# Projections of the prompt begun on four channel chunks, with half of shift and scale

## The reference

```python
mod = (jax.nn.silu(c) @ w_ada + b_ada)[:, None, :]
shift1, scale1, gate1, shift2, scale2, gate2 = jnp.split(mod, N_MOD, axis=-1)
h = rmsnorm(x, g_attn) * (1 + scale1) + shift1
z = h @ w_in
u, q, k, v = jnp.split(z, [D_FOURIER, D_FOURIER + D_NA, D_FOURIER + 2 * D_NA], axis=-1)
```

## Time and profile before

| | before |
| --- | --- |
| median of three runs | 1675.43 us |
| the profiled execution | 1672.69 us |
| its span, first to last instruction | 1670.9 us |
| mean granted TensorE clock | 0.994 of full speed |
| TensorE busy | 1627.1 us, 97% |
| VectorE busy | 1052.8 us, 63% |
| ScalarE busy | 643.7 us, 39% |
| GpSimd busy | 173.1 us, 10% |
| `front`: first matmul of the loop behind the u tiles starts | 139.65 us |

### The profile page before, as it was taken

One profiled execution on the slowest core, in us unless ns is written; L12 is line 12 of the kernel. 1 busy time (PEld: TensorE's weight loads), 2 busy tenths in 40 slices (PEclk: granted clock), 3 DMA queues, 4 the chain that ended last, 5 costly groups with the idle time before them and its releaser, 6 DMA issues.

```text
span 1670.9 us, 20970 instructions
## 1 busy us (share of the span) xinstructions
PE 1627.1 (97%) x7939; PEld 1301.3 (78%) x7939; DVE 1052.8 (63%) x1679; ACT 643.7 (39%) x1121; POOL 173.1 (10%) x123
## 2 busy tenths in 40 slices
PE   5999999999999999999999999999999999999998
PEld 3767888866676888888888888888888877888887
DVE  3524888058968353444664698887878745668774
ACT  4512333158765243433332334333333424343330
POOL 0311222000000232100000000000000001314060
PEclk9999999999999999999999999999999999999999
DMA  9771010433220432543444234333333476767773
GB/s 349 286 239 46 26 38 26 90 59 34 57 89 26 166 137 101 156 137 113 140 135 145 73 120 119 114 96 118 95 95 95 156 266 239 251 221 266 251 249 99
DMA packets 222071, 230.63 MB, mean 138 GB/s; under 512 B 25271, under 2 KB 169873, under 8 KB 221849
## 3 DMA queue, kind: packets, MB, share of 16 engines
q1 hardware_dynamic: 221017, 226.21, 43.0%
q0 software_dynamic: 960, 3.15, 0.5%
HBM read 183.30 MB, written 46.02 MB: 137 GB/s over the span
## 4 chain that ended last, share of the span: by engine, by line
PE 61%; DVE 2%; DMA 2%; SPq 1%; ACT 0%; issue 0%; DVEq 0%; ACTq 0%
PE banks L99 20%; PE banks L101 20%; PE banks L100 20%; DMA a_raw<-fc_rows 1%; PE banks L2405 1%; SPq L1763 1%; DVE a_lo L2210 0%; DVE s_sum L2156 0%; DMA s_raw<-in_w_up 0%; DVE b_lo L2222 0%; DMA s_raw<-in_w_gate 0%; DVE s_lo L2166 0%; SPq L1733 0%; SPq L1744 0%; DMA fc_rows<-s_up 0%
## 5 line engine op out<-in xcount | busy, mean ns | idle before, releaser
L99 PE MATMUL banks<-b_hi,a_hi 128*128 128x512 f32 x462 | 181.8, 394 | 7.9 <-DVE b_lo L2222 4.0
L101 PE MATMUL banks<-b_hi,a_lo 128*128 128x512 f32 x462 | 181.5, 393 | 0.0
L100 PE MATMUL banks<-b_lo,a_hi 128*128 128x512 f32 x462 | 181.3, 392 | 0.0
L99 PE MATMUL banks<-h_hi,p_hi 128*128 128x512 f32 x352 | 138.5, 394 | 0.0
L101 PE MATMUL banks<-h_hi,p_lo 128*128 128x512 f32 x352 | 137.2, 390 | 0.0
L100 PE MATMUL banks<-h_lo,p_hi 128*128 128x512 f32 x352 | 137.0, 389 | 0.0
L99 PE MATMUL banks<-h_hi,s_hi 128*128 128x512 f32 x352 | 136.9, 389 | 0.0
L100 PE MATMUL banks<-h_lo,s_hi 128*128 128x512 f32 x352 | 136.9, 389 | 0.0
L101 PE MATMUL banks<-h_hi,s_lo 128*128 128x512 f32 x352 | 136.9, 389 | 0.0
L99 PE MATMUL banks<-h_hi,win_hi 128*128 128x512 f32 x336 | 132.4, 394 | 3.6 <-DVE h_lo L522 2.8
L101 PE MATMUL banks<-h_hi,win_lo 128*128 128x512 f32 x336 | 131.3, 391 | 0.0
(11 more groups left out here) (263 smaller groups left out, 3404.0 us busy)
## 6 DMA issues: line engine op xcount, KB each, us to landing
a_raw<-fc_rows SPq DMA_DIRECT2D x40, 704.0 KB, 4.6
b_raw<-in_w_down SPq DMA_DIRECT2D x77, 256.0 KB, 5.5
ada_rest<-in_w_ada SPq DMA_DIRECT2D x16, 1024.0 KB, 8.7
b_second<-in_w_down SPq DMA_DIRECT2D x55, 256.0 KB, 6.2
p_raw<-in_w_gate SPq DMA_DIRECT2D x22, 512.0 KB, 3.8
p_raw<-in_w_up SPq DMA_DIRECT2D x22, 512.0 KB, 4.0
s_raw<-in_w_gate SPq DMA_DIRECT2D x11, 1024.0 KB, 5.2
s_raw<-in_w_up SPq DMA_DIRECT2D x11, 1024.0 KB, 5.3
```

The source lines that it names most:

```text
L99: pe.matmul(out, lhs[0], rhs[0], start=start, stop=False)
L100: pe.matmul(out, lhs[0], rhs[1], start=False, stop=False)
L101: return pe.matmul(out, lhs[1], rhs[0], start=False, stop=stop)
```

## The change

The order of the modulation blocks becomes 0, 2, 1, 3, so that shift and scale of channel chunks 0 to 3 are complete after two blocks, and `coef_ready` goes up once for each half. Loads are issued as: x of the prompt in two halves, ada 0, ada 2, w_in 0 and 1, ada 1, w_in 2 and 3, ada 3, then x of chunks 1 and 2. TensorE turns four chunks of the prompt, makes two blocks and their columns (now in banks 6 and 7), turns the other four chunks, then does chunks 0 to 3 of pair 0, block 1, chunk 0 of pair 1, block 3, chunk 1 of pair 1, the two turns of rows, chunks 2 and 3 of pair 1, and then the second halves of pairs 0 and 1. Of the turns of chunk 1 two stand in pair 1 (steps 6 and 7) and six in pair 2 (steps 0 to 5); those of chunk 2 all stand in pair 3. `rest_products(0)` moves from the end of pair 1 to the end of pair 2; blocks 1 and 2 move from pair 2 to pair 3, 3 and 4 to pair 4, 5 and 6 to pair 5, and `mods(7)` stands behind pair 5. The turns of chunk 1 use banks 6 and 7. ScalarE loads the root's table right behind silu; it has `square(4)` ahead of the wait for the second half of the coefficients and of `modulate(4)`, squares 5 to 7 between modulations 5, 6 and 7, and squares 8 and 9 and evacuations 2 and 3 between `modulate(9)` and `modulate(10)`. Semaphore `wf_in` now also counts the second half of x, so a later wait is for 32.

```diff
-            load_x(0)
-            for j in range(AC):
-                sp.dma_start(ada[j][:], w_ada[:, 512 * j:512 * j + 512].rearrange("(k p) n -> p k n", p=128)
-                             ).then_inc(ada_in[j], 16)
-            for r in range(FT):
-                load_u(r)
+            load_x_half(0, x_in[0])
+            load_x_half(1, wf_in)
+            load_ada(0)
+            load_ada(2)
+            load_u(0)
+            load_u(1)
+            load_ada(1)
+            load_u(2)
+            load_u(3)
+            load_ada(3)
             load_x(1)
             load_x(2)
...
+            act.activation(stat[:, 1, 0:1], eps_t[:], ACT.Sqrt)
             for t in range(4):
                 square(t)
             root_x(0)
...
             act.wait_ge(coef_ready, 1)
-            act.wait_ge(parked, KT)
-            for n in range(KT):
-                modulate(n)
+            act.wait_ge(parked, FT)
+            modulate(0)
+            modulate(1)
+            park_x(4)
+            modulate(2)
+            park_x(5)
+            modulate(3)
+            park_x(6)
+            park_x(7)
             split_u(2)
             split_u(3)
-            for t in range(4, 8):
-                square(t)
+            square(4)
+            act.wait_ge(coef_ready, 2)
+            act.wait_ge(parked, KT)
+            modulate(4)
+            modulate(5)
+            square(5)
+            modulate(6)
+            square(6)
+            modulate(7)
+            square(7)
             root_x(1)
             evacuate_u(0)
             evacuate_u(1)
-            for n in range(KT, 2 * KT):
-                modulate(n)
-                if KT + 2 <= n < KT + 6:
-                    square(n - 2)
-            root_x(2)
+            modulate(8)
+            modulate(9)
+            square(8)
+            square(9)
             evacuate_u(2)
             evacuate_u(3)
-            for n in range(2 * KT, 2 * KT + 4):
+            modulate(10)
+            square(10)
+            modulate(11)
+            square(11)
+            root_x(2)
+            for n in range(12, 2 * KT):
                 modulate(n)
...
-            for j in range(AC):
-                pe.wait_ge(ada_in[j], 16)
-                if j >= 2:
-                    pe.wait_ge(mod_row, j - 1)
-                mod_products(ada[j], 6 + j % 2, 0, True, False)
-                mod_products(ada[j][:, 4:8], 6 + j % 2, 4, False, True).then_inc(mod_summed, 1)
-                if j == 0:
-                    for n in range(KT):
-                        turn_x(n)
-                else:
-                    turn_first(j - 1)
-            turn_first(AC - 1)
-            u_pair(0, lambda k: None)
-
-            def during_1(k):
-                turn_x(KT + k)
-                if k == KT - 1:
-                    rest_products(0)
-            u_pair(1, during_1)
+            for n in range(FT):
+                turn_x(n)
+            first_products(0)
+            first_products(1)
+            turn_first(0)
+            turn_first(1)
+            pe.wait_ge(vec_ready, 1)
+            for n in range(FT, KT):
+                turn_x(n)
...
+            u_pair(0, nothing, range(FT))
+            first_products(2)
+            u_pair(1, nothing, range(1))
+            first_products(3)
+            u_pair(1, nothing, range(1, 2))
+            turn_first(2)
+            turn_first(3)
+            u_pair(1, nothing, range(2, FT))
+            u_pair(0, nothing, range(FT, KT))
...
+            def during_1(k):
+                if k >= KT - 2:
+                    if k == KT - 2:
+                        pe.wait_ge(coef_ready, 2)
+                    turn_x(KT + k - 6)
+            u_pair(1, during_1, range(FT, KT))
+
+            def during_2(k):
+                if k < KT - 2:
+                    turn_x(KT + 2 + k)
+                if k == KT - 1:
+                    pe.wait_ge(t_ready, 2 * KT)
+                    rest_products(0)
+            u_pair(2, during_2)
+
+            TURNS_3 = ((0, 1), (2,), (3,), (), (4, 5), (6,), (7,), ())
+
+            def during_3(k):
+                if k == 0:
+                    pe.wait_ge(bank_free, 4)
+                for i in TURNS_3[k]:
+                    turn_x(2 * KT + i)
+                if k % 4 == 3:
+                    mods(1 + k // 4)
+            u_pair(3, during_3)
...
             def during_later(p, k):
-                if p in (2, 3) and k % 2:
-                    if p == 2 and k == 1:
-                        pe.wait_ge(bank_free, 4)
-                    turn_x(2 * KT + 4 * (p - 2) + k // 2)
                 if k % 4 == 3:
-                    m = 2 * p - 3 + k // 4
-                    if m < CHUNKS:
-                        mods(m)
-            for p in range(2, U_TILES // 2):
+                    mods(2 * p - 5 + k // 4)
+            for p in range(4, U_TILES // 2):
                 u_pair(p, lambda k: during_later(p, k))
+            mods(CHUNKS - 1)
             turn_rest(CHUNKS - 1)
             pe.wait_ge(gate_ready, 4)
```

More of the change, by code:

```diff
@@ L159, in front @@
     x = at("x_first", [128, TT, D], F32, X_AT)
-    ada = [at(f"ada{j}", [128, KT, 512], F32, H_LO + 16384 * j if j < 3 else W + 8192) for j in range(AC)]
+    ADA_ORDER = (0, 2, 1, 3)
+    ADA_AT = {0: H_LO, 2: H_LO + 16384, 1: H_LO + 32768, 3: W + 8192}
+    ada = [at(f"ada{j}", [128, KT, 512], F32, ADA_AT[j]) for j in range(AC)]
     park = at("park", [128, KT, T], F32, H_HI)
@@ L364, in _ @@
             store(1)
-            for n in range(KT + 1, 2 * KT, 2):
+            low(9)
+            store(2)
+            store(3)
+            for n in range(11, 2 * KT, 2):
                 low(n)
[L367 to L374, removed]
+            store(4)
+            store(5)
+            for n in range(2 * KT + 1, 3 * KT, 2):
+                low(n)
             for n in range(6, U_TILES):
@@ L391, in square @@
                     act.wait_ge(x_in[t // 4], 16)
+                if t == 2:
+                    act.wait_ge(wf_in, 16)
                 if t:
@@ L462, in _, with park_x @@
             root_x(0)
-            for k in range(KT):
+            def park_x(k):
                 act.wait_ge(x_turned, k + 1)
                 act.activation(park[:, k, 0:CH], banks[:, x_bank(k)], ACT.Copy).then_inc(parked, 1)
+            for k in range(FT):
+                park_x(k)
             split_u(0)
@@ L489, in _ @@
             evacuate_u(5)
-            for n in range(2 * KT + 4, 3 * KT):
+            for n in range(2 * KT, 3 * KT):
                 modulate(n)
@@ L601, in _ @@
             split_u(3)
+            mod_row_of(2)
+            mod_row_of(3)
+            mod_half(1)
+            for n in range(FT, KT):
+                split(n)
             for t in range(4, 8):
                 norm_row(t)
-            for n in range(KT, 2 * KT):
+            for n in range(KT, KT + FT):
                 split(n)
-            for t in range(8, 12):
-                norm_row(t)
+            for n in range(KT + FT, 2 * KT):
+                split(n)
+                norm_row(n - FT)
             mod_rows(0)
             for m in range(1, CHUNKS):
-                for n in (14 + 2 * m, 15 + 2 * m):
-                    if n < 3 * KT:
+                if m < 3:
+                    for n in range(2 * KT + FT * (m - 1), 2 * KT + FT * m):
                         split(n)
@@ L666, in turn_x @@
                 if c == 0:
-                    after(pe, parked, n - 3)
+                    after(pe, parked, n - 5)
                 else:
@@ L680, in mod_products, with first_products, turn_first @@
                 return last
-            def turn_first(j):
-                pe.wait_ge(mod_row, j + 1)
-                for i in range(4):
-                    a = 8 * j + 2 * i
-                    last = pe.matmul(banks[:, 3, a:a + 2], park[:, j % 2, CH + 128 * i:CH + 128 * i + 128], pick[:],
-                                     start=True, stop=True)
+            def first_products(i):
+                j = ADA_ORDER[i]
+                pe.wait_ge(ada_in[j], 16)
+                if i >= 2:
+                    pe.wait_ge(coef_ready, 1)
+                mod_products(ada[j], 6 + i % 2, 0, True, False)
+                mod_products(ada[j][:, 4:8], 6 + i % 2, 4, False, True).then_inc(mod_summed, 1)
+            def turn_first(i):
+                pe.wait_ge(mod_row, i + 1)
+                for t in range(4):
+                    last = pe.matmul(banks[:, 6 + i % 2, 2 * t:2 * t + 2], park[:, i % 2, CH + 128 * t:CH + 128 * t + 128],
+                                     pick[:], start=True, stop=True)
                 last.then_inc(mod_turned, 1)
@@ L713, in turn_rest, with u_pair @@
                     last.then_inc(mod_turned, 1)
-            def u_pair(p, at_step):
-                for k in range(KT):
+            def u_pair(p, at_step, ks=range(KT)):
+                for k in ks:
                     for n in (2 * p, 2 * p + 1):
@@ L807, in _ @@
                     pe.wait_ge(cs_in, 16)
[L808 removed]
```

(1 more changed line is left out.)

58 lines of the change are left out of this document (36 added, 22 removed).

## The result

| | before | changed |
| --- | --- | --- |
| median of 14 runs | 1674.60 us | 1679.35 us |
| range of the runs | 1672.91 to 1677.55 | 1677.24 to 1681.24 |
| ratio to before, 95% interval | | 1.0028 (1.0020 to 1.0035) |
| span of the profiled execution | 1670.9 us | 1679.5 us |
| first projection of the prompt | 39.34 us | 26.88 us |

A forecast was written before the change was run, and what follows sets the result against it. TensorE's own work, busy 97% of the span, was taken as the bound, with only its idle time moving. The terms -4.1 + 5.8 - 0.5 + 1.6 gave +2.8 us, 1675.5 profiled or 1678.2 from the median; range 1672.5 to 1682.0.

The forecast's parts named there:

- rival A: New holes in pair 2: the clock falls, about 1.3 us each; one fall +4.1, two +5.4 us; chance 0.2.
- signs of being wrong: Chunk 4 before 46, pair 2 within 15 us, clock 0.50 after 45, first projection after 31, or last gate under 8.
- Part 1: First half of the prompt: first projection at 27.1 us against 39.34; pair 0's four chunks end at 32.6.
- Part 2: Second half: square(4), waiting for x of chunk 1, holds modulate(4) until 45.5; TensorE's lead shrinks to 4.1 us.
- a wait on the load, not on coefficients: Sign of being right: ScalarE waits for x of chunk 1, about 44 us, before a square ahead of modulate(4).
- Part 3: Pair 2: turns of chunk 1 too close to their use; 5.8 us of new idle time.
- Part 4: Later: wait before chunk 2's turns goes, -0.5 us; modulation blocks 6 and 7 behind the last projection cost +1.6.
- The sum without the clock: Whole change: -4.1 + 5.8 - 0.5 + 1.6 = +2.8 us, with no fall of the clock in the new holes.
- Rival B: First half comes late as loads land out of order; coefficients or weights 4 us late give +4.7 us; chance 0.13.
- C: Pair 2 runs without holes, operands of chunk 1 arriving as fast as taken: -3.0 us, 1672.4; chance 0.12.

The follow-up runs named there:

- e8_warm: The changed kernel with 12 extra matmuls, results unused, in the hole of 2.7 us before products(3); ratio to the kernel before 1.0028.
- e5_load: The changed kernel with the last modulation block loaded ahead of w_in 2 and 3, products(3) done earlier, square(4) still ahead of modulate(4); ratio to the kernel before 1.0032.
- e2_squares: The changed kernel with squares 8, 9 and 10 ahead of modulate(8), in ScalarE's idle time; ratio to the kernel before 1.0031.
- e3_turns: e2_squares with the turns of chunk 1 brought forward to four steps ahead of their use; ratio to the kernel before 0.9987.
- e6_load_sq: e5_load with squares 4 to 7 moved behind modulate(7); ratio to the kernel before 1.0036.
- e4_three: e1_blocks and e3_turns together, on the changed kernel; ratio to the kernel before 0.9979.
- e1_blocks: The changed kernel with modulation blocks 1 to 7 at every third step of pairs 3 to 5, none behind pair 5; ratio to the kernel before 1.0015.
- e9_three_warm: e4_three with 12 extra matmuls in the hole before products(3); ratio to the kernel before 0.9984.
- e10_all_warm: e6_load_sq with e1_blocks' spacing, chunk 1's turns four steps ahead, squares 8 to 11 in idle time, eight extra matmuls before pair 1; 1669.35 us, ratio 0.9969.

## Why the prediction was right

The time, 1679.35 us, lies in the range of 1672.5 to 1682.0, and the holes and the late blocks that should eat up the lead were there. But +4.7 us lies above the forecast's own +0.2 to +4.5, and beyond the 0.2% under which the prediction counted "same" with 0.50; it is among the slower outcomes, which had 0.40. What stood beside the sum is the clock of rival A, and one of the signs of being wrong, a granted clock of 0.50 after 45 us, was seen in this trace.

**Part 1** held: first projection at 26.88 (27.1 forecast), first half of pair 0 done and products(2) begun at 32.89 (32.6).

**Part 2** held in its loads: last block at 39.11 (39.0), x of chunk 1 at 44.22 (44.3). It missed one term: products(3) were priced at 1.92 and took 3.32 at the low clock, so the coefficients came at 46.34 instead of 45.0 and not the square but they were last. `turn(8)` came at 58.92, forecast 58.1; the lead was 3.4 us (free at 61.1, not 60.4) and not 4.1; in e8_warm, without that fall, it was 4.3. I had counted the low clock in the first half, where there was slack, and not at the one place where a wait for a load ended and the path to the end began. That "a wait on the load, not on coefficients" would be seen was wrong for this trace, and right in e5_load and e8_warm.

**Part 3** had the mechanism right and its price 1 us too low. The holes stand at the steps named, and the trace's chains, e2_squares and e3_turns show the cause. Their brackets (0.32, 0.41, 1.18, 0.26, 1.30 and 1.81 us) begin at the end of the matmul before, which lasts 0.39 us against a distance of 0.227. By distances of starts, as the prediction counts (1.83 for a step with a turn, 1.36 without), they are 0.45, 0.64, 1.41, 0.48, 1.53 and 2.09 us, 6.6 together, where 0.5, 0.55, 1.65, 0.6, 1.05 and 1.55 stood, 5.9. The last two are each 0.5 longer since GpSimd took 1.70 us for the low part instead of 1.28, with VectorE scaling a row beside it. For the last:

```profile
78.21 0.75 DVE L552 TENSOR_SCALAR x_first<-x_first,stat 128x1024 f32<-128x1024 f32 x1
...
78.37 1.70 POOL L361 TENSOR_TENSOR h_lo<-t_first,h_hi 128x512 fp32r<-128x512 f32 x1 [3.57 <-DVE h_hi L558]
```

The Trainium skill ("GPSIMD Engine Reference", "8. Key points") says that GpSimd shares its interfaces to SBUF with VectorE and that VectorE instructions in a 2-port mode, or with two inputs in SBUF, contend with it. The trace agrees in that GpSimd's subtraction took 1.70 us beside the scaling at 78.21 and 1.28 at 62.71, with no scaling beside it. In which mode the scaling ran it doesn't show.

**Part 4** held: from the last projection's end, about 136.1, to the loop 9.1 us, 9.2 forecast; the blocks' own share measured 1.2 to 1.3 instead of 1.6.

**The sum without the clock** came out as near as it did partly by luck. e8_warm has the changed kernel's order and no fall before the loop. `rest_products(0)` starts there, and in the kernel before, at

```profile
80.82 1.92 PE L733 MATMUL banks<-ada_rest,silu_pad 128*32 128x512 f32 x16
...
67.47 1.92 PE L678 MATMUL banks<-ada_rest,silu_pad 128*32 128x512 f32 x16
```

By then e8_warm has also done the 48 matmuls of pair 2, 10.9 us, so it is 80.82 - 67.47 - 10.9 = +2.45 us late, where -4.1 + 5.8 = +1.7 was forecast. Behind it, up to the loop, it takes 61.85 us against 61.3 of the same work before: +0.6, where -0.5 + 1.6 = +1.1 was forecast. The two errors cancel to +3.0 beside +2.8.

**Rival A** is what was added. From `turn(8)` to the loop the changed kernel and e6_load_sq took 86.3 us, e5_load and e8_warm 84.7, with the same six holes; the difference is the fall at 80 us in the first two, **1.6 us**. With the fall at 40 us, 1.0 at `turn(8)`, that is 2.6, and +3.0 + 2.6 = +5.6 stands beside the +5.5 of the profiled execution. The median's +4.7 would fit if the second fall came in some executions and not in others; with one trace for the kernel that isn't shown. The chance of 0.2 given to A was too low, because I had compared single holes with the one of 2.78 us in the earlier trace rows; one of 1.81, behind five others, was enough here, and of 1.59, behind a thin stretch of turns, in e6_load_sq.

**Rival B** didn't come: each load landed in its place. **C** couldn't: pair 2 has its holes in every kernel that turns chunk 1 two steps ahead. The gain that was lost is real, though: with the turns and blocks put right, the same early start is 3.5 us below the kernel before (e4_three), the -4.1 - 0.5 of parts 2 and 4 less the 1.0 of the fall at 40 us.

## What to carry to other kernels

Starting a stage earlier gains only as far as the next load allows; work out which load the second half of the stage hangs on before counting the first half's microseconds, and look what stands queued behind a wait on each engine. When work that feeds a stage is moved into that stage, compare the latency of its whole chain (here 2.7 to 3.3 us over three engines, 3.8 where two of them got in each other's way), not its rate, with the distance between issue and use: turns two steps ahead, 2.3 us or less, were too close, four steps ahead left one hole of 0.6 us. Leave no hole of a microsecond or two on TensorE where the path to the end passes; where one can't be avoided, a few matmuls into a free bank kept the clock here, 1.0 to 1.5 us earlier at `turn(8)`. They delay what stands behind them, though, and in none of the three kernels was the total shown to be lower.

## What the runs showed of the hardware

The same holes did and did not bring the clock down. Behind a hole of 1.81 us in pair 2 the granted clock fell to 0.50 in the changed kernel, e2_squares and e6_load_sq, and stayed at 1.00 in e1_blocks, e5_load and e8_warm. A wait of 0.6 to 0.8 us for the last modulation block (e3_turns, e1_blocks) left it at 1.00; 2.69 us (changed), 2.5 us (e2_squares) and 2.4 us (e4_three) didn't. The length of that wait is itself chance: with the same order of loads TensorE went on at 37.9 us in e1_blocks and at 39.1 in the changed kernel. Filling the hole kept it at 1.00 at that place in each of the three kernels in which this was tried. In e8_warm it fell at 143 us, behind three waits of 0.8 us with thin work between them, where it stayed up in all other kernels, those with the same three waits among them (changed, e2_squares, e3_turns, e5_load, e6_load_sq).

The clock falls behind `front` as well: in all twelve traces near 550, 1375 and 1400 us, and in some once or twice more, near 356 us (changed), 446 us (e3_turns, e9_three_warm, e10_all_warm) and 515 to 520 us (e2_squares, e6_load_sq, e9_three_warm). From the start of the loop to the end, in code that no edit touches, the traces take from 1531.3 us (before) to 1536.5 (e3_turns). That is why a microsecond or two at the marks often doesn't show in the ratio.

What the falls cost in the median, beside the profiled executions, stays open: e8_warm takes away the one at 40 us and has the changed kernel's ratio, within an interval of 0.1% to either side, and one profiled execution for a kernel doesn't tell how often a fall comes.
